# A new order of the mixing stage, with memory's projections between the second layer and the second block

## What is computed

```
xn = rms_norm(h, attn_norm_g[layer]);  proj = xn @ w_in[layer]
u_ssm, u_g, v_g, q, k, v = split(proj)
y_ssm  = s5_mixer(u_ssm, ...)          # diagonal state space scan, gelu, glu
y_sgu  = u_g * (W_s rms_norm(v_g) + b) # spatial gating
q = apply_rope(rms_norm(q, q_gain)); k = apply_rope(rms_norm(k, k_gain))
w = softmax(q k1) - lam * softmax(q k2)
y_diff = rms_norm(w v, sub_gain) * (1 - lambda_init)
h = h + concat(y_ssm, y_sgu, y_diff) @ w_out[layer]
h = h + conv_gated_mlp(rms_norm(h, ffn_norm_g[layer]), ...)
# second block: its third branch attends to a memory of 256 rows
kvm = rms_norm_2(mem, g_mem) @ w_mem_kv;  km, vm = kvm[:, :512], kvm[:, 512:]
```

## Time and profile before

| | us |
|---|---|
| median of 3 runs | 1109.61 |
| lowest and highest | 1108.46, 1110.04 |
| the profiled execution | 1109.24 |
| span of its instructions | 1107.0 |
| PE busy | 1017.0 |
| DVE busy | 706.3 |
| ACT busy | 525.9 |
| POOL busy | 273.4 |

### The profile page before, as it was taken

How to read it: one execution, slowest core, us unless ns; L and a number is a source line. 1 busy time by engine, 2 the same in 40 slices (tenths; PEclk the granted TensorE clock), 3 DMA queues, 4 the chain that set the end, 5 groups by cost and what they waited for, 6 DMA issues and landing times.

```text
span 1107.0 us, 15796 instructions
## 1 busy us (share of the span) xinstructions
PE 1017.0 (92%) x6060; PEld 886.6 (80%) x6064; DVE 706.3 (64%) x1140; ACT 525.9 (48%) x869; POOL 273.4 (25%) x276
## 2 busy tenths in 40 slices
PE   6549887899999989978999999989999999999997
PEld 6448776899998877857999998777777888888775
DVE  4865946577896438665677675366556655545594
ACT  6414354465665434363565564254354454444632
POOL 1590300059875001200045440003112200000030
PEclk9868998899999989998899999999999999999999
DMA  9312332555554535323456565554444445544452
GB/s 360 97 58 78 94 114 77 191 173 189 172 181 162 190 122 162 117 76 119 154 179 188 179 185 190 169 179 159 159 134 133 135 151 182 152 133 124 134 171 77
DMA packets 48170, 165.96 MB, mean 150 GB/s; under 512 B 6368, under 2 KB 6752, under 8 KB 48096
## 3 DMA queue, kind: packets, MB, share of 16 engines
q1 hardware_dynamic: 48096, 164.95, 46.9%
HBM read 162.83 MB, written 1.05 MB: 148 GB/s over the span
## 4 chain that ended last, share of the span: by engine, by line
PE 55%; DVE 3%; ACT 1%; POOL 1%; issue 1%; POOLq 0%; DVEq 0%; ACTq 0%
PE PJ L539 10%; PE PJ L541 10%; PE PJ L540 10%; PE PJ L532 4%; PE PJ L533 4%; PE PJ L534 4%; PE T L916 1%; PE PJ L511 1%; PE PJ L510 1%; PE PJ L509 1%; PE S L896 1%; PE S L841 1%; PE T L861 1%; PE T L907 1%; PE T L851 1%
## 5 line engine op out<-in xcount | busy, mean ns | idle before, releaser
L1493 DVE TENSOR_TENSOR wlo<-raw,whi 128x1024 fp32r<-128x1024 f32 x294 | 371.9, 1296 | 158.0 <-ACT whi L985 157.6
L985 ACT ACTIVATE whi<-raw 128x1024 fp32r<-128x1024 f32 x294 | 302.2, 1062 | 68.3 <-DMA raw<-weights_in 62.0
L532 PE MATMUL PJ<-xth,whi 128*128 128x256 f32 x800 | 231.8, 290 | 24.0 <-issue 22.1
L533 PE MATMUL PJ<-xtl,whi 128*128 128x256 f32 x800 | 230.6, 288 | 0.0
L534 PE MATMUL PJ<-xth,wlo 128*128 128x256 f32 x800 | 230.3, 288 | 0.0
L539 PE MATMUL PJ<-whi,xth 128*128 128x512 f32 (+1 forms) x512 | 208.8, 408 | 11.2 <-DVE wlo L1493 9.5
L541 PE MATMUL PJ<-whi,xtl 128*128 128x512 f32 (+1 forms) x512 | 201.3, 393 | 0.0
L540 PE MATMUL PJ<-wlo,xth 128*128 128x512 f32 (+1 forms) x512 | 200.9, 392 | 0.0
L532 PEld LDWEIGHTS PJ<-xth,whi 128*128 128x128 f32 x800 | 158.1, 198 | 26.0 <-issue 24.0
L533 PEld LDWEIGHTS PJ<-xtl,whi 128*128 128x128 f32 x800 | 158.2, 198 | 0.0
L534 PEld LDWEIGHTS PJ<-xth,wlo 128*128 128x128 f32 x800 | 158.0, 197 | 0.0
(11 more groups left out here) (370 smaller groups left out, 1360.8 us busy)
## 6 DMA issues: line engine op xcount, KB each, us to landing
raw<-weights_in SPq DMA_DIRECT2D x294, 512.0 KB, 3.5
rt<-bmerge_in SPq DMA_DIRECT2D x6, 256.0 KB, 3.9
xn<-mem_in SPq DMA_DIRECT2D x2, 512.0 KB, 4.2
xres<-x_in SPq DMA_DIRECT2D x1, 1024.0 KB, 10.0
y_out<-xn SPq DMA_DIRECT2D x4, 256.0 KB, 2.4
rowv<-rows_in SPq DMA_DIRECT2D x1, 576.0 KB, 11.6
cst<-consts_in SPq DMA_DIRECT2D x1, 512.0 KB, 5.4
ptmp<-bexp_in SPq DMA_DIRECT2D x2, 256.0 KB, 9.3
```

Of the source, the lines that this page charges most:

```text
L532: pe.matmul(o, a, xh[:, k, :], start=(first and f % 2 == 0), stop=False, skip_group_check=True)
L533: pe.matmul(o, a, xl[:, k, :], start=False, stop=False, skip_group_check=True)
L985: act.activation(whi[:, p % HIGHS, :], raw[:, p % LOADS, :], ACT.Copy).then_inc(hi_ready, 1)
L1493: dve.tensor_tensor(wlo[:, p % LOADS, :], raw[:, p % LOADS, :], whi[:, p % HIGHS, :].bitcast(F32), ALU.subtract).then_inc(lo_ready, 1)
```

## The change

- The list CHUNKS no longer begins with km and vm; they stand behind the second layer's down products. Within the mixing stage the order is q, k, ssm_u, gmlp, v. A new table STREAM interleaves the halves of the two out groups, and SLOT gives a pair's place in the stream.
- In layer 0 and layer 1 q is multiplied by token tile (`tile_pairs`): all four pairs for the first 128 tokens, then all four for the second. The norm ahead is scaled, transposed and split by tile too (`BY_TILE`); in layer 1 the first tile's transposes stand between the last pairs of the down product.
- q and k are rotated straight out of the accumulator, without their norm. k is scaled afterwards (`k_scaled`), and q's factor is taken into the scale of the exponentials (`hr8`).
- The scan's shuffles and products stand between the pairs of gmlp and behind the scores. In layer 0 `toeplitz_products` come after the third scores, bank by bank in one accumulator, with ACT's copies between.
- The tables of layer 0 are spread: POOL builds the first input table, then the head powers, then the second one and the rest; DVE computes the phase factors in two parts, around k.
- `out_scale` is gone; the softmax's sum enters the norm's epsilon on POOL (`leps`). The factor of the mean in the norms is folded into the gains, so that the reciprocal root takes two POOL operations after the last square instead of three.
- Memory is loaded during layer 1's FFN, its squares and scales are made there, its transposes stand between the two down groups, and km, vm follow around the transposes of the second block's norm.
- The small transfers at the start are split and in another order: x's first tile and the identity come first.

The diff, cut to its core:

```diff
-CHUNKS = [("km", 8, 512), ("vm", 8, 512)]
+CHUNKS = []
 for _l in range(LAYERS):
-    CHUNKS += [(f"ssm_u{_l}", 8, 256), (f"q{_l}", 8, 512), (f"k{_l}", 8, 512), (f"gmlp{_l}", 8, 512),
+    CHUNKS += [(f"q{_l}", 8, 512), (f"k{_l}", 8, 512), (f"ssm_u{_l}", 8, 256), (f"gmlp{_l}", 8, 512),
                (f"v{_l}", 8, 512), (f"out{_l}_0", 8, 512), (f"out{_l}_1", 8, 512)]
     CHUNKS += [(f"up{_l}_{j}", 8, 512) for j in range(UNITS)]
     CHUNKS += [(f"down{_l}_0", FT, 512), (f"down{_l}_1", FT, 512)]
+CHUNKS += [("km", 8, 512), ("vm", 8, 512)]
...
+STREAM = []
+for _n, _k in zip(NAMES, PAIRS):
+    if _n.startswith("out") and _n.endswith("_0"):
+        for _h in range(2):
+            STREAM += [(_n[:-1] + str(_i), 2 * _h + _j) for _i in range(2) for _j in range(2)]
+    elif not _n.startswith("out"):
+        STREAM += [(_n, _j) for _j in range(_k)]
+SLOT = {pair: p for p, pair in enumerate(STREAM)}
...
+            def tile_pairs(name, t, j0, ks, xh, xl, ready=None, between=None):
                 c = chunk(name)
-                for t in range(TT):
-                    for j in range(j0, PAIRS[c]):
-                        p = FIRST[c] + j
-                        if t == 0:
-                            pe.wait_ge(hi_ready, p + 1)
-                            pe.wait_ge(lo_ready, p + 1)
-                        for kk in range(2):
-                            k = 2 * ks[j] + kk
-                            wh, wl = (w[:, p % n, kk * 512:(kk + 1) * 512] for w, n in ((whi, HIGHS), (wlo, LOADS)))
-                            o = PJ[BUF[c]][:, t, :]
-                            h, lw = xh[:, k, t * P:(t + 1) * P], xl[:, k, t * P:(t + 1) * P]
-                            last = j == PAIRS[c] - 1 and kk == 1
-                            pe.matmul(o, h, wh, start=(j == 0 and kk == 0), stop=False, skip_group_check=True)
-                            pe.matmul(o, h, wl, start=False, stop=False, skip_group_check=True)
-                            m = pe.matmul(o, lw, wh, start=False, stop=last, skip_group_check=True)
-                        if t == 1:
-                            m.then_inc(pair_used, 1)
+                for j in range(j0, PAIRS[c]):
+                    p = SLOT[name, j]
                     if t == 0:
-                        m.then_inc(sem("tile0_done"), 1)
+                        pe.wait_ge(hi_ready, p + 1)
+                        pe.wait_ge(lo_ready, p + 1)
+                    if ready is not None:
+                        pe.wait_ge(sem("xt_lo"), ready + 8 * t + 2 * (j + 1))
+                    for kk in range(2):
+                        k = 2 * ks[j] + kk
+                        wh, wl = (w[:, p % n, kk * 512:(kk + 1) * 512] for w, n in ((whi, HIGHS), (wlo, LOADS)))
+                        o = PJ[BUF[c]][:, t, :]
+                        h, lw = xh[:, k, t * P:(t + 1) * P], xl[:, k, t * P:(t + 1) * P]
+                        last = j == PAIRS[c] - 1 and kk == 1
+                        pe.matmul(o, h, wh, start=(j == 0 and kk == 0), stop=False, skip_group_check=True)
+                        pe.matmul(o, h, wl, start=False, stop=False, skip_group_check=True)
+                        m = pe.matmul(o, lw, wh, start=False, stop=last, skip_group_check=True)
+                    if t == 1:
+                        m.then_inc(pair_used, 1)
+                    if between and j == between[0]:
+                        between[1]()
+                return m
...
+                emptied(f"q{l}")
+                if l == 0:
+                    norm_transposes(0, (0,))
+                tile_pairs(f"q{l}", 0, 0, range(4), xth, xtl, ready=32 * l)
+                norm_transposes(2 * l, (1,))
+                tile_pairs(f"q{l}", 1, 0, range(4), xth, xtl, ready=32 * l)
+                if l == 0:
+                    pe.wait_ge(sem("xt_lo"), 16)
+                    b_transposes(0)
+                project(f"k{l}")
+                project(f"ssm_u{l}", fm=True)
+                head_transposes(0, (T0, T1))
+                if l == 0:
+                    pe.wait_ge(sem("bex_ready"), 1)
+                    input_transposes(0, 0, (S0, S1))
+                project(f"gmlp{l}", pairs=[0])
+                shuffle_in()
+                project(f"gmlp{l}", pairs=[1])
+                if l == 0:
+                    pe.wait_ge(sem("bt_ready"), 2)
+                    input_transposes(0, 1, (S0, S1))
+                    project(f"gmlp{l}", pairs=[2])
+                    pe.wait_ge(sem("bt_ready"), 4)
+                    head_transposes(1, (S0, S1))
+                    input_products()
+                else:
+                    head_transposes(1, (S0, S1))
+                    input_products()
+                    project(f"gmlp{l}", pairs=[2])
+                project(f"gmlp{l}", pairs=[3])
                 if l == 0:
...
                 scores(0)
+                project(f"v{l}", pairs=[0])
                 scores(1)
-                project(f"v{l}", pairs=[2, 3])
+                project(f"v{l}", pairs=[1])
+                sgu_products()
+                project(f"v{l}", pairs=[2])
+                prob_transposes(0)
+                project(f"v{l}", pairs=[3])
                 scores(2)
-                for s, n in EMPTIED[f"gmlp{l}"]:
-                    pe.wait_ge(sem(s), n)
-                prob_transposes(0)
-                pe.wait_ge(sem("wst_ready"), l + 1)
-                pe.wait_ge(sem("da_exp"), 16 * l + EXPS[1])
-                for h in range(4):
-                    m = pe.matmul(T0[:, h * P:(h + 1) * P], wsts[:, h, :], md_vn(h), start=(h == 0), stop=True,
-                                  skip_group_check=True)
-                m.then_inc(sem("sgu_done"), 1)
-                for s, n in EMPTIED[f"v{l}"]:
-                    pe.wait_ge(sem(s), n)
+                if l == 0:
+                    for b in range(2):
+                        pe.wait_ge(sem("da_pt"), 1)
+                        if b:
+                            pe.wait_ge(sem("mt_ready"), 4)
+                        toeplitz_products(0, b, B[:, 1, :])
+                output_products()
...
+                project(f"down{l}_0", xh=hth, xl=htl, ready=(sem("ht_lo"), UNITS * l, 1))
+                if l + 1 == LAYERS:
+                    norm_transposes(4)
+                project(f"down{l}_1", xh=hth, xl=htl, pairs=range(FT // 2 - 4))
+                between = (FT // 2 - 2, lambda: norm_transposes(2, (0,))) if l + 1 < LAYERS else None
+                last_pairs(f"down{l}_1", FT // 2 - 4, range(FT // 2), hth, htl, between)
+            project("km", fm=True, xh=memh, xl=meml, ready=(sem("xt_lo"), 64, 4))
             norm_transposes(5)
-            project("mq", fm=True, ready=(sem("xt_lo"), 40, 2))
+            project("vm", xh=memh, xl=meml)
...
             link(pool.memset(mT[:], 0.0))
             norm_rstd(0)
...
+            pool.wait_ge(sem("par_ready"), 3)
+            amplitude_powers()
+            pool.wait_ge(sem("bex_ready"), 1)
+            input_powers(pool, link, 0, 0, x_tile(0), ptmp)
+            head_powers(0, 0)
+            head_powers(0, 1)
+            input_powers(pool, link, 0, 1, x_tile(1), ptmp)
+            link(pool.tensor_tensor(sp_[:, 20, :], sp_[:, 3, :], sp_[:, 3, :], ALU.mult))
+            link(pool.tensor_tensor(sp_[:, 21, :], sp_[:, 20, :], sp_[:, 20, :], ALU.mult))
+            decay_table(pool, link, 0)
+            pool.sem_inc(sem("decay_ready"), 1)
...
             link(pool.tensor_tensor(skip[:, 0:64], ident[:, 0:64], ident[:, 64:128], ALU.add))
             link(pool.tensor_tensor(skip[:, 0:32], skip[:, 0:32], skip[:, 32:64], ALU.add))
             link(pool.tensor_copy(ident4.rearrange("p (t h) -> p t h", t=STEP), wide(skip[:, 0:32], STEP)))
...
             folded(0)
...
+            output_powers(pool, link, 0, 0, ptmp)
+            gate_power(0)
+            output_powers(pool, link, 0, 1, ptmp)
             replicate_inputs(0)
...
+                def rotary(i, src_, terms, done):
+                    co, si = heads8(qn[:, :, :]), heads8(sm[:, 0, :, :])
+                    dve.tensor_tensor(co, heads8(src_[:, :, :]), wide(ropeq[:, 2 * i, :, :], 8, 2), ALU.mult).then_inc(sem(terms), 1)
+                    dve.tensor_tensor(si, heads8(src_[:, :, :]), wide(ropeq[:, 2 * i + 1, :, :], 8, 2), ALU.mult).then_inc(sem(terms), 1)
+                    dve.wait_ge(sem(terms), 2 * (l + 1))
+                    o8 = heads8(xn[:, :, 512 * i:512 * i + 512])
+                    dve.tensor_tensor(o8[:, :, :, 0:32], co[:, :, :, 0:32], si[:, :, :, 32:64], ALU.subtract).then_inc(sem(done), 1)
+                    dve.tensor_tensor(o8[:, :, :, 32:64], co[:, :, :, 32:64], si[:, :, :, 0:32], ALU.add).then_inc(sem(done), 1)
+                    dve.wait_ge(sem(done), 2 * (l + 1))
...
+                head_sums(0)
+                rotary(0, A, "q_terms", "q_rot")
+                if l == 0:
+                    phase_factors(dve, link, 0, pow1)
+                lo_upto(s0 + 9)
...
+                if l == 0:
```

(32 more changed lines are left out.)

976 lines of the change are left out of this document (500 added, 476 removed).

## The result

The changed kernel takes 1114.62 us (median of 4, 1114.15 to 1117.21) against 1109.03 before (1108.09 to 1110.04). The ratio is 1.0058, with a 95% interval of 1.0043 to 1.0072: it is slower by 0.6%, where 1105.7 and faster was forecast. The profiled execution took 1114.15 us with a span of 1112.2, against 1109.24 and 1107.0.

The account below looks back on a forecast made before the run. PE was taken to bound the kernel: 1109.24 - 8.1 (gaps) - 0.5 (clock) + 11 (contention) - 0.5 - 1.3 - 4.2 - 0.3 (rest) = 1105.3 us, or 1105.7 against the median; range 1090 to 1122.

Parts of the forecast that it names:

- Gaps without contention: PE's waits in layer 0's mixing stage, DVE and POOL not disturbing each other: 43.1 us against 51.2, so -8.1.
- a late second tile: At layer 0's start: if x's second tile came late, waits would grow from 14.6 to 17 us, 2.4 lost.
- Contention: Layer 0's stage: POOL's tables beside DVE's steps hold each other up on PE's path, +11 us, bounds 0 to +30.
- the walk: Pair-by-pair count of PE's waits in layer 0's new order, using durations from the profile before: 43.1 us.
- The clock: Low granted clock of PE after long gaps in layer 0's stage: -0.5 us, bounds -4 to +4.
- out0 later than 182 us: Sign of being wrong: layer 0's out products end after 182 us, then the change is slower; about 175 was expected.
- the granted clock through the first 175 us: Sign of being wrong: PE's granted clock below 0.85 from the start to 175 us.
- The rest: After out0: layer 1's stage -0.5, entries to the two FFNs -1.3, second block's entry -4.2, kernel's tail -0.3 us.
- Rival 2: DVE and POOL alternate through layer 0's stage: +30 us instead of +11, clock +2, 1127 us; chance 0.22.
- Rival 1: Contention hardly bites, as POOL's operations fall in DVE's waits: 1095 us; chance 0.27.
- Rival 3: Gaps move to the next queue, DVE before each v pair: -8.1 shrinks to -3, 1111 us; chance 0.13.

Follow-up runs that it names:

- e10_entry_bare: Changed kernel with the transposes of the second block's norm ahead of km, not between km and vm: 1119.56 us, ratio 1.0109 to the kernel before.
- e2_no_tables: Changed kernel without POOL's input tables, folded coefficients and output tables of layer 0, their tiles set to a constant: 1102.15 us, ratio 0.9939 to the kernel before.

## Why the prediction was wrong, point by point

- **Gaps without contention, -8.1.** Right in sum, 43.1 forecast and 43.9 measured for the gaps that it named, and mostly in place. Forecast and measured: pair 6 8.7 and 8.35, pair 9 4.5 and 4.58, the first gate before v 0.7 and 0.65 (the second, 0.5, has no row), pair 16 3.9 and 2.75, Toeplitz 5.1 and 5.16, 1.6 and 1.83, out 2.1 and 2.01, 1.4 and 1.40. The start was 14.6 and is 8.54 + 1.18 + 2.10 + 1.44 + 1.42 + 2.49 = 17.2; the 2.4 that were named as the price of a late second tile came. Two of these in the timeline of PE:

```profile
49.17 0.77 PE L590 MATMUL PJ<-whi,xth 128*128 128x512 f32 x1 [8.35 <-DVE wlo L1612]
...
64.48 0.55 PE L583 MATMUL PJ<-xth,whi 128*128 128x256 f32 x1 [4.58 <-DVE wlo L1612]
```

- **Contention, +11.** The mechanism was right and the size of its waits nearly: three waits that the walk did not have, 2.53 and 2.75 us before pairs 11 and 12 and 5.66 before the gating product, add up to 10.9, and taking the tables away is worth 9.2 us of waits. Of the places where they were put (pairs 5, 9 and 10, `k_scaled` and the phase tables, the scan) only the scan shows in a wait of PE. The first rotation and the scan beside the second output powers were given 2.6 us; the scan alone costs 3.8, and it was forecast as one of two meetings of DVE steps when it is a long pair of instructions. That `gate_power` would hold the tables back until then was not seen; it is the queue that a moved wait stands in front of.
- **The clock, -0.5.** This is the step that failed, and it alone turned the sign. I counted stretches, six before and five after, with some 2.2 us for each. One fewer would be -2.2, and the -0.5 that I took has no working. The five that I named (the start, pairs 6, 9 and 16, Toeplitz) cost 3.8 + 2.3 + 1.5 + 2.9 + 2.0 = 12.5 us, less than the 14.4 of the six before. What I had not counted are three more, 9.8 us: 1.6 and 3.1 behind the waits before pairs 11 and 12, which contention opened and for which that term had a price in waits but none in clock, and 5.1 from 142.5 to 152.75 us, when PE was busy with the output products and what follows them. The term measured +7.7. With it the forecast's sum gives 1113.9 against the median, and the result is 1114.62. Of the signs of being wrong, out0 later than 182 us came true (186.5), and the granted clock through the first 175 us is 0.85, at the bound that was named.
- **The whole q against tiles.** Not a term of the forecast, which took the tile order as given at 14.6 us of waits. The part cost 4.0 us in the time, 7.7 in the traces up to the end of out0.
- **The rest, -6.3.** Measured -6.9 in the profiled execution. The entry to the second block is the large part of it and was shown by e10_entry_bare. Layer 1's stage was not tested by itself, and it takes 3 us more or less from one trace to another with the same code there, so that the two numbers agree so well is in part luck.
- **The rivals.** Rival 2, slower by contention in every step, had the right sign and the wrong mechanism: waits are 55 us, not 73. Rival 1 is excluded by e2_no_tables. Rival 3 said that the gaps move, at a price of 5 us; gaps did appear in new places, but those before pairs 11 and 12 and the gating product go when the tables go, so they are contention.

## What to carry to other kernels

When an order is changed on an engine that waits, count for each gap not only its length but the low clock behind it. In the changed kernel a low stretch cost 1.5 to 3.1 us beyond the gap ahead of it, and the gap before the second Toeplitz half, with the short wait that followed it, 7.1. A wait that contention opens brings such a stretch too, so it wants a price in both terms. A long wait on a queue that also carries table work holds that work back until it collides with somebody else, so a step that waits goes behind the ones that don't. And the few idle microseconds that are left can be filled with products that nobody reads: 44 of them at one place gave 7.8 us here. Last, look at more than one execution: 3 us of a trace can be a stretch of low clock in a stage that nobody touched.
